# A two-layer model block: a new order of tiles in the last mixers, a merged set-up, weights made ready early, and a swapped product in the forgetting attention

## The chip, the cores and the metric

The kernel runs on one core of a Trainium2 chip. The metric is the device time of one execution in microseconds (us). A profile holds one execution. TensorE is called PE (its weight loads PEld), VectorE DVE, ScalarE ACT, GpSimd POOL, and SyncE, which here issues the DMAs, SP.

## What is computed

Two blocks over one sequence of 2048 tokens, model width 1024, all float32. The first block projects the input to 4652 columns, runs five mixers (spatial gating, forgetting attention, mLSTM, RWKV-7, memory attention) and projects back. The second projects to 3784 columns, runs two mixers and ends with a projection, a residual and a layer norm. What the change touches, from the reference:

```python
# forgetting attention, per block of 128 queries and head
s = einsum("bthd,bshd->bhts", qb, k) * scale + fb[..., :, None] - big_f[..., None, :]
p = softmax(where(k_pos <= q_pos, s, -inf));  out = einsum("bhts,bshd->bthd", p, v)
...
# second block, sparse attention, per block of 128 queries
dots = einsum('bqhd,bsd->bqhs', iqb, ik) * idx_scale               # index scores, 8 heads
score = einsum('bqh,bqhs->bqs', iwb * w_scale, relu(dots))         # -inf where not admissible
_, sel = top_k(score, 256)
logits = einsum('bqhr,bqkr->bqhk', ql, c_sel) * scale + bias;  o = einsum(softmax(logits), c_sel)
# second block, HGRN2, scanned over chunks:  o and state from q, k, v, cumulated log gates
...
y = einsum('bsc,cd->bsd', concatenate([o_a, o_b]), w_o)
x = layer_norm(ALPHA * x + y, ln_g, ln_b)
```

## The kernel before

**Steps.** The program is a row of blocks (`step`), each with a barrier of all engines at its end. Inside a step the work is written as branches, and each branch is a generator per engine that yields places between 0 and 1. `together` merges the branches of one engine by these places into one fixed order. An engine works in that order strictly, so an instruction that waits holds up everything of its engine that stands behind it. SP's order is written in the same way; waits for stores of the step before stand at its head.

**The last mixers** (`second_mixers`, line 3296). The sequence is 16 tiles of 128 queries. Tile t sees the keys of tiles 0 to t, so its cost grows with its width W = 128 (t+1). Four parts follow one another for each tile, each in a later step:

- `index_scores`: per index head and piece of 512 keys a matmul (L2651), a Relu on ACT (L2635) and a multiply-add on DVE (L2614), in two PSUM banks in turn.
- `upper_half`, on DVE alone: sixteen rounds that bisect the upper 16 bits of the 256th largest score, each a counting pass over W (L2714) and two small operations. Tiles 0 and 1 have no more than 256 keys and skip it.
- `lower_half`: sixteen rounds on ACT for the lower 16 bits, each a Sign pass over W with a sum (L2754) and two small ones; then on DVE, from place 0.66 on and behind a wait for ACT's last round (L2773), a chain of passes over W that makes the selection mask (L2774 to L2804).
- `attend`: logits (L2995), masked sum and maximum on DVE (L2933), exponentials on ACT, transposes (L3001), their copies on ACT, and the weighted sum (L3008) for 4 heads; at the end a product with w_uv and a gate.

Beside them `hgrn_chunk` works one chunk of the HGRN in steps 0 to 15, forwards in time, a long chain over all engines (seven levels, POOL, ACT, PE and DVE in turn).

Tiles go from 15 down to 0. Step k has index 15-k, upper half 16-k, lower half 17-k and attention 18-k, so 19 steps work, and a 20th stores the last rows. Buffers for scores rotate by `k % 3`, the others by `k % 2`. Before the loop stand a load step, a step that norms c, forms the table of relative biases and transposes c and the index keys (L3330 to L3369), two steps for the HGRN's lower bound (`hgrn_setup`), one that sets a constant, and one that waits for the first tiles. The bias table is loaded from memory in step 0 and mirrored by four matmuls in step 1.

**The last projection** (`project_out` with a layer norm, line 2323) loads w_o in 8 pieces of 128 rows through three slots and splits each into a high and a low part (L2461 on ACT, L2484 on DVE). Each output tile takes 48 matmuls (L2417 to L2419) of 128x512. The first two tiles are computed piece by piece as the weights come. On SP the columns of the third tile are queued behind all the weights' loads.

**The forgetting attention** (`fox_attend`, line 1199) runs for one tile of queries per step beside the two halves of an RWKV chunk, whose triangular inverse (L2154, blocks of 64x64) is the last thing in most steps. Per head and piece of 512 keys: logits (L1298), maximum on DVE (L1272), Exp on ACT, 128x128 transposes (L1315), copies (L1257), and in `weigh` (L1322) the product of the transposed probabilities (stationary, 128x128) with the values (moving, 128x64), summed in PSUM.

## Time and profile before

| | |
|---|---|
| median of 3 runs | 5283.35 us |
| lowest, highest | 5280.79, 5286.9 us |
| profiled execution | 5289.84 us |
| its span | 5288.2 us |
| busy share PE / DVE / ACT / POOL | 83% / 51% / 36% / 13% |
| granted TensorE clock, mean | 0.827 |

A busy share is a mean over stages. Whether an engine sets the time has to be read stage by stage: from a table of busy times in a stretch, and from what stands idle before an instruction and what released it. The timeline view merges neighbouring instructions of a kind into one row; the time from one row's start to the next one's start is what these instructions cost on their engine. A matmul of float32 has two records, a transpose one.

### The profile page before, as it was taken

Reading aid. Unit: us, or ns where it says so; the run is one execution under the profiler, and the core shown is the slowest. Engines: PE = TensorE matmul, PEld = TensorE weight load, DVE = VectorE, ACT = ScalarE, POOL = GpSimd, SP = SyncE. Lnnn points to the kernel's source line nnn. Section 1 sums busy time; section 2 is a strip of 40 time slices with the busy share of each in tenths; the row PEclk is TensorE's granted clock in tenths of the full one; section 3 lists DMA queues with packets and bytes.
Section 4 is the critical chain, followed back from the end, with each engine's and each line's share of the span. In section 5 each row is a group of like instructions: output and inputs, shape, how many; then the busy total and the mean of one; then the engine's idle time right before and its main releaser. Section 6 shows DMA issues by size and latency. Waiting matters only on the chain. (4 is left out here: it accounts for less than half of the span.)

```text
span 5288.2 us, 65270 instructions
## 1 busy us (share of the span) xinstructions
PE 4384.3 (83%) x23498; PEld 3313.7 (63%) x23498; DVE 2679.4 (51%) x5418; ACT 1921.6 (36%) x3904; POOL 712.9 (13%) x745
## 2 busy tenths in 40 slices
PE   7997899983578888898899999956688887876679
PEld 6876777772466666676787888833344444544567
DVE  3114444454555544544212111138988888887546
ACT  3112232333323323333102010113677767777621
POOL 3111111100000000000000000012223333434400
PEclk9998999985677767767899999976577887878779
DMA  5337666653000000000423212120000001011033
GB/s 181 117 120 240 206 219 216 200 183 129 28 23 24 23 23 23 23 12 5 166 96 115 82 68 76 55 61 23 18 19 19 19 19 37 19 37 37 24 126 116
DMA packets 203971, 426.38 MB, mean 81 GB/s; under 512 B 37544, under 2 KB 67916, under 8 KB 203484
## 3 DMA queue, kind: packets, MB, share of 16 engines
q1 hardware_dynamic: 203648, 422.20, 23.2%
q8 instruction: 187, 3.06, 0.2%
q14 instruction: 136, 1.11, 0.1%
HBM read 300.47 MB, written 121.65 MB: 80 GB/s over the span
## 5 line engine op out<-in xcount | busy, mean ns | idle before, releaser
L3162 POOL TENSOR_TENSOR ds_E<-ds_bT 128x256 f32<-128x256 f32 x112 | 72.9, 651 | 2869.0 <-ACT ds_bT L3131 2683.6
L2651 PE MATMUL ds_big<-ds_ikT,ds_iqT 64*128 64x512 f32 (+3 forms) x640 | 378.0, 740 | 90.2 <-ACT ds_iqT L2628 56.5
L301 PE MATMUL g_acc<-g_ws_hi,g_hT_hi 128*128 128x512 f32 (+1 forms) x1024 | 386.9, 378 | 0.0
L303 PE MATMUL g_acc<-g_ws_hi,g_hT_lo 128*128 128x512 f32 (+1 forms) x1024 | 385.3, 376 | 0.0
L302 PE MATMUL g_acc<-g_ws_lo,g_hT_hi 128*128 128x512 f32 (+1 forms) x1024 | 385.2, 376 | 0.0
L2714 DVE TENSOR_SCALAR_CACHE_REDUCE ds_eq<-ds_hi,ds_num 128x2048 uint16<-128x2048 uint16 (+13 forms) x224 | 331.3, 1479 | 25.7 <-issue 3.5
L529 PE MATMUL mm_big<-mm_gw_hi,mm_ghT_hi 128*128 128x512 f32 (+1 forms) x768 | 318.5, 415 | 30.4 <-PEq L134 30.4
L530 PE MATMUL mm_big<-mm_gw_lo,mm_ghT_hi 128*128 128x512 f32 (+1 forms) x768 | 300.2, 391 | 0.0
L531 PE MATMUL mm_big<-mm_gw_hi,mm_ghT_lo 128*128 128x512 f32 (+1 forms) x768 | 300.2, 391 | 0.0
L2754 ACT ACTIVATE ds_signs<-ds_lo,ds_at 128x2048 bf16<-128x2048 uint16 (+13 forms) x224 | 291.3, 1300 | 1.2
L328 DVE COPY g_stage<-g_acc 128x512 f32<-128x512 f32 (+1 forms) x64 | 41.5, 649 | 459.2 <-PE g_acc L303 459.2
L2651 PEld LDWEIGHTS ds_big<-ds_ikT,ds_iqT 64*128 64x128 f32 x640 | 110.9, 233 | 238.3 <-issue 83.7
L2614 DVE SCALAR_TENSOR_TENSOR ds_score<-ds_rel,ds_iw,ds_score 128x512 f32<-128x512 f32 (+3 forms) x280 | 227.6, 817 | 62.6 <-ACT ds_rel L2635 43.2
L1298 PE MATMUL fox_big<-fox_kT,fox_qT 65*128 65x512 f32 (+3 forms) x320 | 223.0, 791 | 25.5 <-PEq L134 25.5
L2635 ACT ACTIVATE ds_rel<-ds_big 128x512 f32<-128x512 f32 (+3 forms) x320 | 167.6, 528 | 189.7 <-PE ds_big L2651 89.6
L3270 PEld LDWEIGHTS ds_big<-ds_E 128*128 128x128 f32 x896 | 137.4, 234 | 140.0 <-issue 74.8
L1257 ACT ACTIVATE fox_pT<-fox_big 128x512 f32<-128x512 f32 (+3 forms) x160 | 85.2, 533 | 371.5 <-PE fox_big L1315 371.4
L347 ACT ACTIVATE g_stage<-g_acc 128x512 f32<-128x512 f32 (+1 forms) x64 | 36.2, 565 | 502.5 <-PE g_acc L303 502.5
L303 PEld LDWEIGHTS g_acc<-g_ws_hi,g_hT_lo 128*128 128x128 f32 x1024 | 193.8, 189 | 35.5
L302 PEld LDWEIGHTS g_acc<-g_ws_lo,g_hT_hi 128*128 128x128 f32 x1024 | 193.9, 189 | 34.8
L301 PEld LDWEIGHTS g_acc<-g_ws_hi,g_hT_hi 128*128 128x128 f32 x1024 | 194.0, 189 | 34.7
L3270 PE MATMUL ds_big<-ds_E 128*128 128x128 f32 x896 | 158.7, 332 | 67.1 <-POOL ds_E L3169 39.4
(512 smaller groups left out, 10307.8 us busy)
## 6 DMA issues: line engine op xcount, KB each, us to landing
mm_ghT_hi<-turned SPq DMA_DIRECT2D x96, 512.0 KB, 4.1
mm_ghT_lo<-turned SPq DMA_DIRECT2D x96, 512.0 KB, 5.4
proj<-g_stage SPq DMA_DIRECT2D x112, 256.0 KB, 2.0
proj<-mm_gstage SPq DMA_DIRECT2D x80, 256.0 KB, 5.0
mm_x<-proj SPq DMA_DIRECT2D x64, 256.0 KB, 3.9
second_raw<-in_w_in SPq DMA_DIRECT2D x56, 256.0 KB, 4.1
proj<-fp_stage SPq DMA_DIRECT2D x48, 256.0 KB, 2.0
mm_graw<-in_w_in SPq DMA_DIRECT2D x40, 256.0 KB, 6.5
```

Source lines behind the costliest of these rows:

```text
L301: pe.matmul(sums, hT.hi[:, k, tile], wt.hi[:, k, 0:width], start=(k == 0), stop=False)
L302: pe.matmul(sums, hT.hi[:, k, tile], wt.lo[:, k, 0:width], start=False, stop=False)
L303: mm = pe.matmul(sums, hT.lo[:, k, tile], wt.hi[:, k, 0:width], start=False, stop=(k == KD - 1))
L529: pe.matmul(sums, b.hT.hi[:, u % 3, k], wt.hi[:, k, 0:width], start=(k == 0), stop=False)
L530: pe.matmul(sums, b.hT.hi[:, u % 3, k], wt.lo[:, k, 0:width], start=False, stop=False)
L531: m = pe.matmul(sums, b.hT.lo[:, u % 3, k], wt.hi[:, k, 0:width], start=False, stop=(k == KD - 1))
L1298: pe.matmul(big[:, n, 0:wd], b.qT[:, h, k * P:(k + 1) * P], b.kT[:, h, x:x + wd], start=True, stop=True).then_inc(s.logits, 1)
L2614: d = dve.scalar_tensor_tensor(out=score[:, x:x + wd], in0=rel[:, n % 2, 0:wd], scalar=sg, in1=score[:, x:x + wd], op0=ALU.mult, op1=ALU.add)
L2651: pe.matmul(big[:, n % 2, 0:wd], iqT[o, h // 2], b.ikT[o, x:x + wd], start=True, stop=True)\
L2714: dve.tensor_scalar(seen, hi, cand, 0.0, ALU.is_ge, ALU.add, accum_out=count)
L2754: act.activation(signs, lo, ACT.Sign, bias=now, accum_out=sums[:, bit:bit + 1])
L3270: m = pe.matmul(big[:, 6 + l % 2, h * P:(h + 1) * P], E[:, l % 2, h], E[:, l % 2, h], start=True, stop=True)
```

## The change

1. **Order of tiles.** `ATTENDED = [1, 0, 9, 15, 3, 14, 4, 13, 5, 12, 6, 11, 7, 10, 8, 2]`; `SCORED` is the same without tiles 1 and 0, which take all their keys and are no longer scored. Step k has index SCORED[k] (k < 14), upper half SCORED[k-1], lower half ATTENDED[k], attention ATTENDED[k-1]. From the third entry on lower half and attention are those of SCORED[k-2] and SCORED[k-3]. 17 steps work and an 18th stores. Buffers rotate by the place in the order (`PLACE`).
2. **Set-up.** One step (`last_mixers_setup`) does what the load step and the five steps behind it did; the copy of the transposed index keys moves from DVE to ACT, in two halves. The bias table's load and its mirroring are both in step 0.
3. **Weights of the last projection.** In step 16, beside the attention of tile 2, `last_weights` loads and splits w_o into buffers that take the place of the index, threshold and HGRN buffers. `project_out` gets them as `held`, leaves out its own loads and asks for columns and rows at once.
4. **Forgetting attention, k >= 4.** `weigh` has the values as the stationary operand (64 columns) and the probabilities as the moving one (128 columns). Even key tiles sum in partitions 0 to 63, odd ones in 64 to 127 of PSUM bank 7. At the end ACT copies the sums, and four matmuls with a fold matrix (two identities one above the other) add the halves and turn them back.

```diff
+FOLDED = 4
@@ fox_attend
+        if folded:
+            yield 11 / N
+            act.wait_ge(s.f_weighed, HEADS * NP)
+            act.activation(pT[:, 0], sums, ACT.Copy).then_inc(s.f_sums_kept, 1)
...
+        if folded:
+            yield 11 / N
+            take(pe, "o")
+            pe.wait_ge(s.f_sums_kept, 1)
+            for h in range(HEADS):
+                m = pe.matmul(o[:, h], pT[:, 0, h], b.fold[:], start=True, stop=True)
+            m.then_inc(s.f_folded, 1)
...
+            at = x // P + t
+            v, w = b.v[:, at, h * HD:(h + 1) * HD], pT[:, (h * NP + p) % 2, t]
+            if folded:
+                m = pe.matmul(sums[(LOW, HIGH)[at % 2], h], v, w, start=(at < 2), stop=(at + 2 > k))
+            else:
+                m = pe.matmul(o[:, h], w, v, start=(at == 0), stop=(at == k))
@@ the order
+SCORED = [9, 15, 3, 14, 4, 13, 5, 12, 6, 11, 7, 10, 8, 2]
+ATTENDED = list(range(PLAIN - 1, -1, -1)) + SCORED
+PLACE = {t: n for n, t in enumerate(ATTENDED)}
@@ last_mixers_setup, PE
+            pe.wait_ge(s.ik_in, 32)
+            for t in range(8):
+                m = pe.transpose(big[:, 5 + t // 4, (t % 4) * P:(t % 4 + 1) * P],
+                                 ik[:, t].rearrange("p r d -> p (r d)"), c.ident)
+            m.then_inc(s.ik_t, 1)
+            pe.wait_ge(s.oh_in, 32)
+            for k in range(5):
+                m = pe.matmul(big[0:HEADS, k], rb, oh[:, k * 512:(k + 1) * 512], start=True, stop=True)
+            m.then_inc(s.biases, 1)
+            pe.wait_ge(s.bias_kept, 1)
...
@@ last_weights
+        for k in range(D_MODEL // P):
+            yield 0.01 * k
+            if k >= 3:
+                sp.wait_ge(s.pw_lo, k - 2)
+            sp.dma_start(b.x[:, k % 3], w_out[k * P:(k + 1) * P, :]).then_inc((s.pw_in0, s.pw_in1, s.pw_in2)[k % 3], 16)
...
+            yield 0.1 + 0.11 * k
+            act.wait_ge((s.pw_in0, s.pw_in1, s.pw_in2)[k % 3], 16 * (k // 3 + 1))
+            act.activation(b.ws.hi[:, k], b.x[:, k % 3], ACT.Copy).then_inc(s.pw_hi, 1)
...
+            yield 0.15 + 0.11 * k
+            dve.wait_ge(s.pw_hi, k + 1)
+            dve.tensor_tensor(b.ws.lo[:, k], b.x[:, k % 3], b.ws.hi[:, k].bitcast(F32), ALU.subtract)\
+               .then_inc(s.pw_lo, 1)
@@ second_mixers
-        order = list(range(TILES - 1, -1, -1))
-        for k in range(TILES + 4):
+        for k in range(TILES + 2):
+            if k == TILES:
+                early.close()
+                last.x = B.sb("px", [P, 3, D_MODEL])
+                last.ws = Split(B, "pws", [P, D_MODEL // P, D_MODEL])
...
+                if k < N:
+                    branches.append(index_scores(c, ib, s, proj, big, order[k]))
+                if 1 <= k <= N:
+                    branches.append(upper_half(c, tb, s, order[k - 1]))
+                if k < TILES:
+                    branches.append(lower_half(c, tb, s, attended[k]))
+                if 1 <= k <= TILES:
+                    branches.append(attend(c, ab, s, proj, big, attended[k - 1], after))
+                if k == TILES:
+                    branches.append(last_weights(last, s, w['w_o_2']))
```

## Rows read from the trace of the kernel before

**Rows 1.** The page: granted TensorE clock in tenths, 40 slices of the span.

```profile
PEclk9998999985677767767899999976577887878779
```

**Rows 2.** Stages: stretch, length, busy PE, PEld, DVE, ACT, POOL, clock, DMA share, GB/s.

```profile
3464.30:3523.00 58.70, 13.91 (x42) 6.08 (x42) 24.58 (x18) 1.58 (x3) 0.00 (x0) 0.57 0.32 79
3523.00:5060.80 1537.80, 1163.53 (x4712) 707.90 (x4712) 1255.70 (x2468) 1015.58 (x2081) 533.25 (x608) 0.76 0.07 25
5063.40:5288.20 224.80, 197.82 (x896) 163.49 (x896) 125.92 (x168) 35.09 (x73) 0.00 (x0) 0.93 0.37 136
1598.10:2504.00 905.90, 798.91 (x6240) 609.89 (x6240) 443.50 (x1104) 286.11 (x540) 0.00 (x0) 0.72 0.06 19
```

**Rows 3.** Same view: loop steps 0, 1, 3, 3 to 12, 15, 16.

```profile
3523.00:3590.10 67.10, 51.74 (x176) 25.79 (x177) 39.53 (x55) 32.60 (x65) 30.38 (x34) 0.78 0.10 36
3590.10:3695.10 105.00, 70.00 (x184) 34.11 (x184) 91.25 (x134) 32.45 (x64) 29.68 (x34) 0.61 0.05 16
3803.60:3928.90 125.30, 107.66 (x420) 61.62 (x420) 113.11 (x189) 88.57 (x156) 34.69 (x38) 0.76 0.05 18
3803.60:4796.90 993.30, 793.17 (x3356) 481.26 (x3357) 873.27 (x1706) 715.22 (x1408) 339.37 (x380) 0.80 0.07 24
4934.40:4996.50 62.10, 41.79 (x204) 31.83 (x204) 29.53 (x66) 44.23 (x120) 31.58 (x38) 0.75 0.09 30
4996.50:5022.20 25.70, 19.48 (x64) 13.60 (x64) 6.57 (x22) 8.39 (x17) 3.98 (x4) 0.53 0.12 41
```

**Rows 4.** Same view: step 3 split at DVE's start on the lower half.

```profile
3803.60:3896.20 92.60, 80.32 (x256) 42.08 (x257) 82.61 (x144) 74.53 (x123) 27.51 (x33) 0.69 0.07 24
3896.20:3928.90 32.70, 27.33 (x167) 19.54 (x164) 30.50 (x47) 14.04 (x33) 7.18 (x6) 0.96 0.00 1
```

**Rows 5.** Lines 2754, 2774 in step 3: ns min/median/max, first and last start.

```profile
L2754 ACT ACTIVATE ds_signs<-ds_lo,ds_at x16: 1879/1886/1907, 3810.0 to 3882.2; 128x1920 bf16<-128x1920 uint16 x16
...
L2774 DVE CAST ds_num<-ds_kept x1: 142/142/142, 3896.2 to 3896.2; 128x1 uint16<-128x1 f32 x1
```

**Rows 6.** Group by line and shape, loop: busy us, mean ns, idle before.

```profile
L2714 DVE TENSOR_SCALAR_CACHE_REDUCE ds_eq<-ds_hi,ds_num 128x2048 uint16<-128x2048 uint16 x16 | 37.5, 2346 | 1.8 <-issue 0.2
```

**Rows 7.** Line 1322, steps k>=4: PE, PEld, clock; PE's timeline, k=15.

```profile
1598.10:2504.00 905.90, 149.98 (x1008) 148.03 (x1008) 0.72 0.06 19
...
2462.95 1.00 PE L1322 MATMUL fox_big<-fox_v,fox_pT 128*128 128x64 f32 x8
2463.79 0.65 PE L1298 MATMUL fox_big<-fox_kT,fox_qT 65*128 65x512 f32 x1
...
2475.72 0.60 PE L1315 MATMUL fox_big<-consts_sb,fox_L 128*128 128x128 f32 x4
2476.16 1.00 PE L1322 MATMUL fox_big<-fox_v,fox_pT 128*128 128x64 f32 x8
2477.09 0.68 PE L2154 MATMUL fox_big<-fox_X,fox_G 64*64 64x64 f32 x16
2477.70 0.70 PE L1298 MATMUL fox_big<-fox_kT,fox_qT 65*128 65x512 f32 x1
...
2499.26 0.68 PE L2154 MATMUL fox_big<-fox_ex,fox_XT 64*64 64x64 f32 x16
2499.77 0.63 PE L2154 MATMUL fox_big<-fox_XT,fox_ex 64*64 64x64 f32 x16
```

**Rows 8.** Set-up: landing of ct's load; timeline row of the reciprocal.

```profile
DMA to landing us min/median/max: 7.8/7.8/7.8
...
3511.06 3.35 DVE L3058 RECIPROCAL ds_lb<-ds_lb 128x512 f32<-128x512 f32 x1
```

**Rows 9.** Timeline: start us, length, engine, line; first products of last projection.

```profile
5072.98 0.79 PE L2417 MATMUL pf_acc<-pf_ws_hi,pf_mS_hi 128*128 128x512 f32 x1 [0.56 <-DVE pf_mS_lo L2478]
...
5087.84 0.80 SPq L2367 DMA_DIRECT2D pf_x<-x  x2
...
5094.42 1.97 PE L2411 MATMUL pf_tp<-consts_sb,pf_m 128*128 128x128 f32 x8 [8.57 <-DMA pf_m<-mixed]
```

More of the change, by code:

```diff
@@ L1078, in fox_rwkv_and_gating @@
         fb.qT, fb.kT, fb.v, fb.z = qT, kT, v, B.sb("z", [P, 2, GW])
+        fb.fold = B.sb("fold", [P, HD])
         rb = rwkv_early_buffers(B)
@@ L1083, in fox_rwkv_and_gating @@
             ub = sgu_buffers(nc, c, E, w)
-            with step(nc, "sgu_in gains_in ahead_in turned masked scaled cleared") as (block, s):
+            with step(nc, "sgu_in gains_in ahead_in turned masked scaled cleared folds") as (block, s):
                 @block.sync
@@ L1105, in _ @@
                     dve.memset(carry[:], 0.0).then_inc(s.cleared, 1)
+                    dve.tensor_tensor(fb.fold[:], c.ident[:, LOW], c.ident[:, HIGH], ALU.add).then_inc(s.folds, 1)
                     dve.wait_ge(s.gains_in, 48)
@@ L1205, in fox_attend @@
     NP = len(PIECES)
-    o = big[:, 7, 0:GW].rearrange("p (h d) -> p h d", h=HEADS)
+    sums = big[:, 7].rearrange("p (h t) -> p h t", h=HEADS)
+    folded = k >= FOLDED
     N = 12.0
@@ L2458, in _ @@
                 keep(0)
-                for k in range(K):
+                if held:
+                    keep(1)
+                for k in range(0 if held else K):
                     act.wait_ge(w_in[k % 3], 16 * (k // 3 + 1))
@@ L2481, in _ @@
                 rest(0)
-                for k in range(K):
+                if held:
+                    rest(1)
+                for k in range(0 if held else K):
                     dve.wait_ge(s.w_hi, k + 1)
@@ L2526, with bias_flip @@
 BIAS_SIGNALS = "bias_in flipped flip_kept "
-def bias_load(bias, s, table):
+def bias_flip(c, bias, s, big, table):
     def sync(sp):
@@ L2670, in threshold_buffers @@
     return b
-def threshold_setup(nc, b):
-    with step(nc, "start_set") as (block, s):
-        @block.vector
-        def _(dve):
-            dve.memset(b.at[:, 2:3], -32767.5).then_inc(s.start_set, 1)
 SELECT_SIGNALS = "low_found "
@@ L2695, in upper_half @@
     cand, hit, n_hi = (cell(n) for n in range(3))
-    top, need, level = (b.kept[:, k % 2, n:n + 1] for n in range(3))
+    top, need, level = (b.kept[:, PLACE[k] % 2, n:n + 1] for n in range(3))
     KEEP = float(TOPK)
@@ L2871, in sync @@
         sp.dma_start(gate[:].rearrange("p h d -> p (h d)"), proj[tok, E_G:E_G + H * P]).then_inc(s.g_in, 16)
-        if k:
-            n = attend_loads(b, sp, s.q_ahead, proj, k - 1)
+        if after is not None:
+            n = attend_loads(b, sp, s.q_ahead, proj, after)
             yield 1.0
@@ L3301, in second_mixers @@
+LAST_SIGNALS = "pw_in0 pw_in1 pw_in2 pw_hi pw_lo "
+def second_mixers(nc, c, w, proj, mix, table, onehot, x_old, out):
     H, R, KEEP = 4, 128, float(TOPK)
+    order, attended, N = SCORED, ATTENDED, len(SCORED)
     with ExitStack() as ctx:
@@ L3450, in _ @@
                     together(pe, "tensor", branches)
+        banks.close()
+        project_out(nc, c, mix, w['w_o_2'], x_old, out, "pf", ln=(w['ln_g_2'], w['ln_b_2']), held=last)
 def program(nc, t, consts, onehot, out):
```

324 lines of the change are left out of this document (165 added, 159 removed).

## Prediction

> **What bounds the kernel now.** I read the page's clock line first: the granted TensorE clock changes from stage to stage, so this is a chain of stages with limits of their own [rows 1]. Then the table by stage [rows 2]: the set-up of the final mixers takes 58.7 us, their loop 1537.8 with DVE busier than PE (1255.7 against 1163.5), the last projection 224.8, and the forgetting-attention steps that the change touches 905.9, of which PE is busy 798.9. Then the loop by its steps [rows 3], which I number 0 to 18 (a store step of 2.6 us follows). In steps 1 to 12 DVE is busy all but some 10 to 14 us, as 113.1 of 125.3 in step 3, or 873.3 of 993.3 in steps 3 to 12 together. Steps 0 and 15 have little for DVE (39.5 and 29.5) and still take 67.1 and 62.1: a floor which the chain of one HGRN chunk sets. Steps 16 to 18 do nothing but the attention of tiles 2, 1, 0; the last two end the loop and take 38.6 us together [rows 2, 3]. Last, step 3 split at the instruction with which DVE takes up the lower half [rows 4, 5]: before it DVE is busy 82.6 of 92.6 us, behind it 30.5 of 32.7. ACT had ended its 16 passes at 3884 (the last starts at 3882.2), 12 us before DVE came to them at 3896.2. ACT's chain is covered by DVE's own work, by 12 us, and the new order spends that margin.
>
> **A model of one step, tried on the old ones.** DVE takes a step's work in a written order: the whole upper half, two thirds of the rest, then the lower half's tail among the last third. So a step is the later of two prefixes plus a suffix. I added the durations of each branch's instructions in every step; they are nearly linear in the tile number t. DVE: upper half 21 (t=2) to 53 us (15), lower half 7 to 15, index 8 (t=0) to 31, attention 5 to 16, HGRN 10.3. ACT: lower half 22 (t=2) to 44, index 3 to 20, attention 6 to 21, HGRN 16.3. The counting passes carry most of the slopes: 16 of 2.35 us on DVE for tile 15 [rows 6], 16 of 1.89 on ACT for tile 14 [rows 5]. With R the sum of index, attention and HGRN on an engine: DVE prefix = upper + 0.66 R + 5; ACT prefix = lower + 0.60 R + 3; suffix = DVE's lower + 0.34 R + 1.5. The constants are read off the splits of the old steps. For old step 3 that is 88.2 + 34.4 = 122.6 against 125.3, for steps 3 to 12 together 992 against 993.3 [rows 3].
>
> **The loop in its new order.** Step k has index SCORED[k], upper half SCORED[k-1], lower half SCORED[k-2], attention SCORED[k-3]. So wide upper half and wide attention meet in even steps, wide index and wide lower half in odd ones. Even, step 4 (index 4, upper 14, lower 3, attention 15): DVE prefix 51.7 + 27 + 5 = 83.7, ACT prefix 53.6, suffix 22.5: 106.2. Odd, step 5 (index 13, upper 4, lower 14, attention 3): DVE prefix 25.6 + 28.5 + 5 = 59.1, but ACT prefix 42.6 + 25.6 + 3 = 71.2. So DVE stands 12 us at the lower half, with index sums, HGRN picks and attention queued behind it; suffix 31.6: 102.8. Steps 2, 3 and 6 to 14 give by the same sum 96.8, 111.4, 104.7, 102.0, 104.4, 97.7, 102.2, 97.5, 102.9, 85.9, 75.5. Step 1 is DVE's sum of 87 us and the 10 by which old step 1 is over its own: 97. Steps 0 and 15 are at the floor, 64 and 66 [rows 3]. Steps 0 to 15 make 1517. The attention of tiles 1 and 0 lies in steps 1 and 2 at no cost of its own, and the index of tiles 0 and 1 is gone; the price is that DVE waits for ACT in odd steps and that both ends are thinly filled. Step 16 has the attention of tile 2 (25.7 [rows 3]) beside the last weights. In the last projection these were done 24 us after its start (5063.4 to 5087.84, where SP's wait for them ends [rows 2, 9]). Here they start some 4 us late, behind the store wait at the head of SP's queue, and share ACT and DVE: I take 34.5, between 28 and 42. Loop: 1551.5 against 1537.8, **+14 us**. Bounds: -19 if ACT's prefix never binds (every step its DVE sum plus 6.5 us, the mean excess of old steps 3 to 12), +35 if the even steps also run out of PE in their short suffix: PE is busy 27.3 of 32.7 us behind the split of step 3 [rows 4], and a suffix of 22.5 us must hold nearly the same attention.
>
> **The set-up** becomes one step; before it was two rounds of loads, three short steps and a round of arrivals. ct lands at about 11.6 us (issued third, 7.8 us to land as before [rows 8]). PE forms the bias table from 16 to 24.6, DVE copies it by 27.4, the transposes of ct end at 33, their copy at 35.6, and the lower bound's chain behind it (a reciprocal of 3.35 [rows 8] and five short ones) near 42. With the block's edges 43: **-16 us**, between -22 and -10. The flips of the bias table move from step 1 into step 0, whose 64 has them.
>
> **The last projection** starts with its weights ready. PE's first product came at 5072.98, 9.6 us into the step, and later PE stood 8.57 us until 5094.42, since the third tile's columns were queued on SP behind all weight loads [rows 9]. The second stall goes whole, of the first 2.5 us, and less idle time means fewer products at the low clock. **-12 us**, between -15 and -8. What is late next is PE itself, 197.8 us [rows 2].
>
> **The forgetting attention** changes for k of 4 and more: 12 steps, 504 products of probabilities and values, 1008 PE records, PE busy 150.0 us with them [rows 7]. Each now loads 64 columns of weights and streams 128, and neighbours write to different halves of the partitions. At the full clock 8 records of the old form take 0.84 us and 4 transposes, which stream 128 columns, 0.44 [rows 7]: 105 to 110 ns a record either way. So if nothing runs side by side there is no gain, and if pairs do, half. No row shows two column halves over all 128 rows. The nearest is L2154, 64 x 64 blocks on the diagonal: 16 records in 0.51 us [rows 7], 32 ns each, where half of 110 is needed to stream 64 columns alone. I take full overlap: -75. Against it: the last matmul of an odd count runs alone (+4). Each of 144 groups changes the array's shape twice: entering costs 0.09 us (8 records 0.93 ahead of L2154, 0.84 ahead of L1298), leaving 0.10 (L2154 0.61 instead of 0.51) [rows 7]: +29. The closing fold has 8 more records a step (+14), and its wait for ACT's 0.6 us copy stands ahead of the last inverse levels, which end the step (+6). Net -22 on PE, which is busy 88% of the stage: **-19 us**, between -55 (switches hidden) and +46.
>
> The Trainium skill speaks on both sides here. Its page TensorEngine Tiling (Array Packing), section Performance Considerations, advises this very exchange of stationary and streaming operand with two column tiles where the streamed dimension is 64 or less; by it the term would stay as above. Its page TensorE: Matmul & The Clock Gate, section The mechanism, says that a weight load overlaps running matmuls only where the row group differs; by it the term would be that of the first rival. No row here shows this shape.
>
> **Sum.** -16 + 14 - 12 - 19 = -33. The profiled execution took 5289.84 us, its span is 5288.2; less 33 that is 5257. The median of the three runs is 5283.35, so the forecast is **5250 us**, 0.6% faster.
>
> **Rivals.**
> First, the column halves do not run side by side, because both load and stream over the same 128 rows. For: the only concurrent rows differ in row half too. Against: L2154's blocks also write to different column halves and lose nothing by it. Price: the gain of 75 goes, the switches, folds and waits remain, +46 instead of -19, total 5315, slower. It decides from a pitch of about 96 ns a record in the mean of both clocks (today 149): above that the edit loses. Chance 0.15.
> Second, ACT's prefix stays hidden and each step is DVE's sum plus 6.5: loop -19, total 5217. For: ACT's work in step 5 (85 us) fits into 91. Against: DVE waits at one fixed place of its order. Chance 0.18.
> Third, the alternation costs more: in even steps PE ends the suffix, in odd ones both engines lose: loop +35, total 5271. For: PE at 27.3 of 32.7 [rows 4]. Chance 0.17.
> Fourth, the change doesn't do what it says: the small tiles lengthen steps 1 and 2 by what they took alone, 5283. Against: DVE needs 5 us for each, beside 80 of other work. Chance 0.04.
> The forecast: 0.46.
>
> **Range and chances.** The forecast's own range is 5222 to 5276. With the second and third rival and a part of the first, 8 in 10 is 5200 to 5305. A measurement of this kernel can tell about 0.2% from no change: faster means under 5272.8, slower over 5293.9. Faster 0.74 (forecast 0.44, second 0.18, third 0.10, the rest 0.02), same 0.12, slower 0.14.
>
> **What would show it.** In the loop, DVE idle some 12 us ahead of the lower half in step 5, released by ACT, and even steps near 104. The set-up one step of about 43. In the last projection the first product within 7.5 us and no stall at the third tile. In the forgetting attention, records of the weighted sum in pairs, their PE time near 75, the stage near 887. I am wrong if that time stays near 150, if DVE is busy throughout odd steps, or if step 16 is over 42.

## The result, and the profile after

The changed kernel takes 5312.78 us (median of 5 runs, 5307.27 to 5314.62) against 5283.35 us (5 runs, 5280.16 to 5290.55): a ratio of 1.0052, with a 95% interval of 1.0038 to 1.0067. It is slower by half a per cent. I had forecast 5250 us, with a range of 5200 to 5305. The result is outside that range and on its other side.

The stages, as in [rows 2] (columns: stretch, length, busy PE, PEld, DVE, ACT, POOL, clock, DMA share, GB/s): set-up, loop, last projection, and the twelve forgetting-attention steps with k of 4 and more.

```profile
3460.30:3501.90 41.60, 16.31 (x42) 7.51 (x42) 22.39 (x17) 3.43 (x6) 0.00 (x0) 0.51 0.45 112
3501.90:5096.50 1594.60, 1189.81 (x4672) 721.99 (x4672) 1237.42 (x2448) 1019.13 (x2071) 532.60 (x608) 0.73 0.08 27
5099.10:5311.20 212.10, 193.77 (x896) 160.44 (x896) 116.23 (x160) 26.85 (x65) 0.00 (x0) 0.95 0.33 124
1604.10:2501.00 896.90, 766.87 (x6336) 536.17 (x6336) 442.52 (x1104) 291.91 (x552) 0.00 (x0) 0.73 0.06 19
```

| stage | before | after | difference | forecast |
|---|---|---|---|---|
| set-up | 58.7 | 41.6 | -17.1 | -16 |
| loop | 1537.8 | 1594.6 | +56.8 | +14 |
| last projection | 224.8 | 212.1 | -12.7 | -12 |
| forgetting attention, k >= 4 | 905.9 | 896.9 | -9.0 | -19 |
| all else | | | +5.0 | 0 |
| span | 5288.2 | 5311.2 | +23.0 | -33 |

Two stages came out as worked out, one gave half of its gain, and the loop alone turned the sign. What is under "all else" is in stages that the change does not touch: step k = 4 of the forgetting attention began at 1598.1 us before and at 1604.1 after, and between 1594 and 1613 us over the profiles of this study.

In the loop DVE has 18 us less to do than before (1237.4 against 1255.7) and the loop is 57 us longer. So it is waiting that grew: DVE is idle for 357.2 us of the loop, where it was idle for 282.1. The same view by steps, against [rows 3]: steps 0, 4, 5 and 16, and step 5 split at the instruction with which DVE takes up the lower half.

```profile
3501.90:3572.60 70.70, 57.77 (x168) 29.31 (x168) 32.16 (x53) 26.69 (x56) 26.71 (x34) 0.64 0.10 34
3883.70:3993.80 110.10, 79.80 (x388) 53.01 (x388) 93.58 (x173) 61.49 (x140) 33.58 (x38) 0.81 0.06 22
3993.80:4108.90 115.10, 91.59 (x252) 48.54 (x252) 82.20 (x165) 77.90 (x144) 33.40 (x38) 0.60 0.06 21
5064.10:5096.50 32.40, 17.42 (x64) 11.73 (x64) 14.92 (x28) 15.94 (x25) 5.96 (x4) 0.63 0.46 154
3993.80:4074.90 81.10, 67.84 (x154) 33.27 (x154) 52.73 (x124) 67.27 (x116) 25.55 (x32) 0.52 0.09 30
4074.90:4108.90 34.00, 23.75 (x99) 15.28 (x98) 29.47 (x43) 10.63 (x28) 7.84 (x7) 0.80 0.00 0
```

The even step 4 is a step as DVE had them before: busy 93.6 of 110.1. The odd step 5 is not: DVE is busy 82.2 of 115.1, and 28 us of its idle time lie before the lower half. There I had expected one wait of 12 us, right at the lower half. The two instructions in question, in step 5 (durations in ns min/median/max, first and last start), as in [rows 5]:

```profile
L2783 ACT ACTIVATE ds_signs<-ds_lo,ds_at x16: 1879/1886/1897, 4000.2 to 4063.3; 128x1920 bf16<-128x1920 uint16 x16
...
L2803 DVE CAST ds_num<-ds_kept x1: 150/150/150, 4074.8 to 4074.8; 128x1 uint16<-128x1 f32 x1
```

ACT's last pass starts at 4063.3 and its chain is over at 4065.9, 72.1 us into the step; I had worked out 71.2. DVE comes to the lower half only at 4074.8, 9 us later, and nothing holds it there. It is late because it had been held earlier. The waits of step 5 (engine, line waited for, us in total, times, longest), first DVE's, then ACT's:

```profile
DVE ds_score L2652 <- ACT ds_rel L2673: 13.5, 9, 3.2
DVE ds_score L2656 <- ACT ds_rel L2673: 5.2, 2, 3.9
```

```profile
ACT ds_rel L2673 <- PE ds_big L2689: 14.2, 7, 3.4
ACT ds_rel L2673 <- DVE ds_score L2652: 7.0, 5, 3.7
```

The index branch is a chain over three engines: PE forms a product (L2689), ACT takes its Relu (L2673), DVE adds it to the scores (L2652, L2656), through two PSUM banks and two SBUF places. In odd steps the index is wide (tiles 14, 13, ...) and so is the lower half, whose Sign passes stand on ACT between the Relus. A few microseconds of step 5, in order of time (start, length, engine, line; in brackets the idle time before it and who ended it):

```profile
4010.30 2.07 PE L2689 MATMUL ds_big<-ds_ikT,ds_iqT 64*128 64x512 f32 x2
...
4013.99 0.59 ACT L3122 ACTIVATE ds_kT<-ds_big 128x512 f32<-128x512 f32 x1
...
4014.47 1.89 ACT L2783 ACTIVATE ds_signs<-ds_lo,ds_at 128x1920 bf16<-128x1920 uint16 x1
...
4017.31 0.60 ACT L2673 ACTIVATE ds_rel<-ds_big 128x512 f32<-128x512 f32 x1
...
4017.94 0.49 DVE L2656 TENSOR_SCALAR ds_score<-ds_rel,ds_iw 128x512 f32<-128x512 f32 x1 [3.95 <-ACT ds_rel L2673]
```

The product is there at 4012.4 (one product is two records). ACT takes its Relu at 4017.3. Ahead of it in ACT's order stand work of the HGRN chunk (a table load of 1.28 us and three short instructions, of which the last is shown) and a Sign pass of 1.89 us with its short followers. DVE stands 3.95 us for it. Over the whole loop the waits of the index sums for a Relu more than doubled. First before, then after:

```profile
DVE ds_score L2614 <- ACT ds_rel L2635: 43.2, 28, 3.8
...
DVE ds_score L2618 <- ACT ds_rel L2635: 7.7, 6, 3.8
```

```profile
DVE ds_score L2652 <- ACT ds_rel L2673: 90.3, 60, 4.0
...
DVE ds_score L2656 <- ACT ds_rel L2673: 19.5, 8, 4.2
```

That is 50.9 us before and 109.8 after: 59 of the 75 us by which DVE's idle time grew. In steps 3, 5, 7, 9 and 11 together DVE waits 62.2 us for Relus, in steps 4, 6, 8, 10 and 12 10.0 us; in the loop before, the same steps had 8.6 and 3.6.

### The profile page after: what moved, and what is told of

The parts are those of the page before. It is cut to its first block and busy times, and to the rows that moved or that the text cites. A ratio compares the mean times of both kernels' runs of the same rounds, so it can differ in the third digit from the quotient of the medians.

```text
span 5311.2 us, 65208 instructions
## 1 busy us (share of the span) xinstructions
PE 4382.9 (83%) x23554; PEld 3258.4 (61%) x23554; DVE 2646.5 (50%) x5390; ACT 1924.2 (36%) x3900; POOL 714.0 (13%) x745
## 5 line engine op out<-in xcount | busy, mean ns | idle before, releaser
L2689 PE MATMUL ds_big<-ds_ikT,ds_iqT 64*128 64x512 f32 (+3 forms) x608 | 393.8, 793 | 75.2 <-ACT ds_iqT L2666 55.6
L2743 DVE TENSOR_SCALAR_CACHE_REDUCE ds_eq<-ds_hi,ds_num 128x1280 uint16<-128x1280 uint16 (+13 forms) x224 | 331.3, 1479 | 25.0 <-issue 2.6
L2783 ACT ACTIVATE ds_signs<-ds_lo,ds_at 128x1280 bf16<-128x1280 uint16 (+13 forms) x224 | 291.3, 1300 | 1.4
L2652 DVE SCALAR_TENSOR_TENSOR ds_score<-ds_rel,ds_iw,ds_score 128x512 f32<-128x512 f32 (+3 forms) x266 | 210.0, 791 | 106.2 <-ACT ds_rel L2673 90.3
L3264 PEld LDWEIGHTS ds_big<-ds_E 128*128 128x128 f32 x896 | 149.6, 251 | 159.0 <-POOL ds_E L3163 81.7
L3264 PE MATMUL ds_big<-ds_E 128*128 128x128 f32 x896 | 170.1, 349 | 72.5 <-POOL ds_E L3163 44.5
L2689 PEld LDWEIGHTS ds_big<-ds_ikT,ds_iqT 64*128 64x128 f32 x608 | 108.3, 241 | 196.5 <-issue 73.6
L2673 ACT ACTIVATE ds_rel<-ds_big 128x512 f32<-128x512 f32 (+3 forms) x304 | 162.9, 538 | 174.3 <-PE ds_big L2689 123.8
L301 PEld LDWEIGHTS g_acc<-g_ws_hi,g_hT_hi 128*128 128x128 f32 x1024 | 193.8, 189 | 34.8
```

Of the source, the lines that this page charges most:

```text
L301: pe.matmul(sums, hT.hi[:, k, tile], wt.hi[:, k, 0:width], start=(k == 0), stop=False)
L2652: d = dve.scalar_tensor_tensor(out=score[:, x:x + wd], in0=rel[:, n % 2, 0:wd], scalar=sg, in1=score[:, x:x + wd], op0=ALU.mult, op1=ALU.add)
L2689: pe.matmul(big[:, n % 2, 0:wd], iqT[o, h // 2], b.ikT[o, x:x + wd], start=True, stop=True)\
L2743: dve.tensor_scalar(seen, hi, cand, 0.0, ALU.is_ge, ALU.add, accum_out=count)
L2783: act.activation(signs, lo, ACT.Sign, bias=now, accum_out=sums[:, bit:bit + 1])
L3264: m = pe.matmul(big[:, 6 + l % 2, h * P:(h + 1) * P], E[:, l % 2, h], E[:, l % 2, h], start=True, stop=True)
```

## The experiments

All kernels below are the changed kernel with one edit or two. The kernel before was run on the same chip beside each group; its medians there were 5291.6 (first four), 5292.4 (next four) and 5287.6 us (last four), and a ratio is against those. Where no interval or range is given (experiments 2, 3, 5 and 6, and the first run of 7), the time is that of one execution, and every figure of a stage or step is that of one profile.

**1. The change taken apart: order and fold.** The first run leaves the forgetting attention in its old form, the second gives the fourteen scored tiles in falling order as before the change (tiles 1 and 0 still ahead of them), the third does both.

```diff
-FOLDED = 4
+FOLDED = 16
```

> The changed kernel with the forgetting attention as before (FOLDED = 16, nothing else). Theory A (the loop alone makes the kernel slower, the fold still earns a little): the 12 attention steps go from 896.9 back to some 906, the total rises by 5 to 20 us over the changed kernel, to 5318 to 5333. Rival B (the fold costs what it saves on PE, since the inverse's chain and the fold's own wait end the step, and the clock falls): the total moves by less than 8 us either way. Rival C (the fold is the loss): the total falls by 10 to 30 us and the changed kernel without it is as fast as before.

```diff
-SCORED = [9, 15, 3, 14, 4, 13, 5, 12, 6, 11, 7, 10, 8, 2]
+SCORED = list(range(TILES - 1, PLAIN - 1, -1))
```

> The changed kernel with the tiles scored from wide to narrow, 15 down to 2, behind tiles 1 and 0 (SCORED descending, nothing else), so that the small tiles still fill the early steps but no wide index meets a narrow upper half. Theory A (the alternation is the loss: in odd steps DVE waits for Relus in the index ring): steps 3 to 13 return to the lengths of before (1066 us together), the loop with its step 16 is 1510 to 1525 us instead of 1595, the total 5225 to 5245, ratio to before 0.989 to 0.993. Rival B (the filled early steps and the merged buffers are the loss, not the alternation): the loop stays above 1570 and the total within 20 us of the changed kernel.

> Both edits: descending order and no fold. If the two parts add up, the total is that of the descending order plus what the run without the fold shows against the changed kernel. Theory A: 5235 to 5260. Rival B (the fold costs what it saves): within 8 us of the descending order alone. Rival C (the fold is a loss): 10 to 30 us below it.

("fox" is the forgetting attention with k of 4 and more.)

| | new fold | old form |
|---|---|---|
| alternating order | 5312.8 (loop 1594.6, fox 896.9) | 5327.5 (1594.4, 910.0) |
| falling order | 5239.0 (1526.6, 896.9) | 5246.6 (1526.6, 910.0) |

Ratios: no fold 1.0079 (1.0058 to 1.0101), falling order 0.9899 (0.9881 to 0.9918), both 0.9930 (0.9906 to 0.9953). The alternation costs 68 us of loop, and the rest of the change (small tiles in the early steps, short set-up, weights loaded early, fold) is worth 1% with the old order. Over all profiles of this study the alternating loop took 1594.4 to 1598.6 us (three) and the falling one 1512.3 to 1526.6 (four), so that 68 is at the low end. By the medians the fold earns 8 us in the falling order and 15 in the alternating one, where the two kernels were run in different groups (against their own medians of the kernel before it is 6.5). The intervals with and without it overlap in both orders, and its stage, 13 us shorter here, was not always so (experiment 7). The loop in falling order:

```profile
3498.20:5024.80 1526.60, 1181.38 (x4672) 712.68 (x4672) 1242.22 (x2448) 1017.43 (x2071) 534.23 (x608) 0.75 0.08 28
```

DVE's sum for the loop is the same within 5 us in both orders (1237.4 and 1242.2), ACT's within 2. The order moves no work, it only moves waiting: at L2652 DVE waits 52.4 us for Relus in the falling order (41.0 in a second profile), 90.3 in the alternating one. Waits for Relus are not all of it. DVE also waits longer for the attention's logits, first in falling, then in alternating order:

```profile
DVE ds_L L2962 <- PE ds_big L3024: 28.2, 24, 3.2
```

```profile
DVE ds_L L2962 <- PE ds_big L3024: 53.0, 32, 5.8
```

That is in steps 14 and 15, where the alternating order has the attention of tiles 10 and 8 and the falling one that of 4 and 3: DVE waits 39 us for logits there against 7, and the two steps take 145.2 us against 123.0. This part of the price stood in the forecast (75.5 and 66 us).

**2. How the loss grows with the contrast.** An order that steps down in mild turns.

```diff
-SCORED = [9, 15, 3, 14, 4, 13, 5, 12, 6, 11, 7, 10, 8, 2]
+SCORED = [15, 9, 14, 8, 13, 7, 12, 6, 11, 5, 10, 4, 3, 2]
```

> The changed kernel with the order 15, 9, 14, 8, 13, 7, 12, 6, 11, 5, 10, 4, 3, 2 after tiles 1 and 0: alternation with a width difference of six tiles instead of up to twelve. Theory A (the loss grows with the mismatch of wide index and lower half against the narrow upper half): the loop is between the descending order's 1526.6 us and the alternation's 1594.6, near 1560. Rival B (a constant cost of alternating, or of the first steps): 1590 or more. Rival C: as the descending order, 1535 or less.

Measured 5284.41 us, loop 1562.1: about halfway between 1526.6 and 1594.6. So a milder contrast between neighbours costs less. DVE's waits for Relus moved with the wide index, which now stands in even steps: 39.7 us in steps 4 to 12, 3.0 in steps 3 to 11.

**3. Is it ACT's Sign passes?** They read 128 keys instead of up to 2048; their number and order stay. This kernel leaves most keys out of the search for the lower 16 bits, so its selection is another.

```diff
-            act.activation(signs, lo, ACT.Sign, bias=now, accum_out=sums[:, bit:bit + 1])
+            act.activation(signs[:, 0:P], lo[:, 0:P], ACT.Sign, bias=now, accum_out=sums[:, bit:bit + 1])
```

> A timing probe on the changed kernel: ACT's sixteen Sign passes of the lower half read only the first 128 keys of a tile instead of all, so the selection is not that of the reference. It takes 12 to 28 us of ACT work out of every step with a wide lower half. Theory A (in odd steps DVE waits for Relus that stand behind the Sign passes in ACT's order): odd steps 3 to 9 fall from 104 to 118 us to their DVE sum plus 5 to 9, that is to 90 to 98, and even steps move by less than 4. Rival B (the Relus are late because PE runs at the low clock and its index products are late): odd steps fall by less than 5 us and DVE still waits 10 us or more for Relus in step 5.

Measured 5257.91 us; the loop falls from 1594.6 to 1538.7. The odd steps 3 to 11 fall from 547.0 together to 503.4, the even steps 4 to 12 stay at 520.3. DVE's waits for Relus in these odd steps fall from 62.2 us to 20.1, which is 42 of the 44 us. So it is the passes that hold up the Relus. By itself the total could not tell this from ACT's own sum, which my formula had and which short passes take away too; that ACT's sum was not the later one is seen in step 5 of the changed kernel, where DVE came 9 us behind its end. But step 5 came to 105.1, not to the 90 to 98 that I expected: only half of the way. Its rows (whole, then up to DVE's start on the lower half), and the waits of DVE and of ACT in it:

```profile
3986.40:4091.50 105.10, 84.78 (x252) 44.81 (x252) 82.81 (x165) 54.46 (x144) 33.09 (x38) 0.66 0.07 23
3986.40:4057.40 71.00, 61.08 (x154) 29.59 (x154) 53.32 (x125) 43.82 (x116) 25.28 (x32) 0.60 0.10 34
```

```profile
DVE ds_score L2652 <- ACT ds_rel L2673: 6.8, 4, 2.5
...
DVE ds_score L2656 <- ACT ds_rel L2673: 1.6, 1, 1.6
```

```profile
ACT ds_rel L2673 <- PE ds_big L2689: 24.1, 13, 3.4
ACT ds_rel L2673 <- DVE ds_score L2652: 7.6, 6, 3.7
```

DVE's waits for Relus fell from 18.7 to 8.4 us, and ACT now waits 24.1 us for products: behind ACT the next link of the chain is PE.

**4. Is it the depth of the ring?** Three banks and three places in steps 3, 5, 7, 9 and 11, with the products issued a turn earlier.

```diff
-    b.rel = B.sb("rel", [P, 2, 512])
+    b.rel = B.sb("rel", [P, 3, 512])
...
-            if n >= 2:
-                act.wait_ge(s.summed, n - 1)
-            act.activation(rel[:, n % 2, 0:wd], big[:, n % 2, 0:wd], ACT.Relu).then_inc(s.relus, 1)
+            if n >= deep:
+                act.wait_ge(s.summed, n - deep + 1)
+            act.activation(rel[:, n % deep, 0:wd], big[:, n % deep, 0:wd], ACT.Relu).then_inc(s.relus, 1)
...
-            yield place(n - 0.4 * (n % 2))
+            yield place(max(0, n - 0.4 * (n % 2) - (deep - 2)))
...
+            deep = 3 if k in (3, 5, 7, 9, 11) else 2
```

> The changed kernel, but in steps 3, 5, 7, 9 and 11 the index products rotate through three PSUM banks and three Relu buffers instead of two (the narrow attention of those steps gets two banks instead of three), and PE issues each product a turn earlier. Theory A (in odd steps PE, ACT and DVE hold one another up because the ring of index products has two places): odd steps 3 to 11 fall from 547 us together by 20 to 40, the total to 5275 to 5295. Rival B (ACT's own sum, with the wide lower half, sets the pace, whatever the ring): odd steps fall by less than 8 us together.

The attention of these steps has two banks instead of three for it. Measured 5306.73 us, ratio 1.0034 (1.0016 to 1.0051); odd steps 540.4, loop 1590.0. A third place gives 6.6 us of the 36 that the odd steps are over the forecast, and DVE's waits for Relus in them stay, 62.5 us against 62.2. Nor is 6.6 us clear of chance: the three kernels that share the alternating loop word for word (the changed one, the one without the fold and the first of experiment 7) had 547.0, 550.5 and 554.1 us in the odd steps, and 519.0 to 520.3 in the even ones.

**5. Is it the length of the products?** The index matmuls in fp32r.

```diff
-    b.iqT = B.sb("iqT", [P, IDX_HEADS // 2, P])
+    b.iqT = B.sb("iqT", [P, IDX_HEADS // 2, P], F32R)
...
-        ikT, score = E.sb("ikT", [P, SEQ]), E.sb("score", [P, 3, SEQ])
+        ikT, score = E.sb("ikT", [P, SEQ], F32R), E.sb("score", [P, 3, SEQ])
```

> A timing probe on the changed kernel: the index products' operands are kept as fp32r, so a product is one pass instead of two; the scores lose precision and the selection can differ from the reference's. Theory A (PE's late products are a part of the ring's time in odd steps, by its low clock): odd steps 3 to 11 fall by 20 us or more together and ACT's wait for products in step 5 falls from 14.2 us below 7. Rival B (only ACT's Sign passes matter, of which the short-Sign probe already took 44 us of 547): less than 8 us together.

Measured 5297.09 us; odd steps 531.5, even 513.3, loop 1566.1. In step 5 PE sheds 27 us and the step 6.4:

```profile
3990.80:4099.50 108.70, 64.34 (x220) 42.20 (x220) 82.16 (x165) 77.98 (x144) 33.05 (x38) 0.62 0.07 22
```

```profile
DVE ds_score L2652 <- ACT ds_rel L2673: 8.9, 7, 3.2
DVE ds_score L2656 <- ACT ds_rel L2673: 5.2, 2, 3.9
```

```profile
ACT ds_rel L2673 <- DVE ds_score L2652: 8.9, 6, 3.7
ACT ds_rel L2673 <- PE ds_big L2689: 3.5, 4, 1.3
```

ACT's waits for products fell from 14.2 to 3.5 us, and DVE still waits 14.1 for Relus: with long Sign passes the products are not what sets the pace. Over the five odd steps DVE's waits for Relus stay, 61.4 us against 62.2; the steps gain 12 of their 15.5 us from other waits, those for logits among them (5.2 to 0). Neither theory was right here, it is in between. Of the 28 us of loop the odd steps gave 15.5, the even ones 7.0 and step 0, where ACT has few passes to make, 5.3 (70.7 to 65.4).

**6. Two links at once.** Short passes with fp32r products, and short passes with the three-place ring.

> The changed kernel in its alternating order, with ACT's Sign passes reading only the first 128 keys (which leaves most keys out of the lower half's search) and the index products in fp32r (which rounds their operands). Odd steps 3 to 11 together took 547.0 us, 503.4 with short Sign passes alone, 531.5 with fp32r alone. Theory A (the chain product, Relu, sum runs at the pace of its slowest link: ACT while its Sign passes are long, PE behind it): the two together do more than their sum of -59, near 480 us, and in step 5 ACT's waits for products, 24 us with short passes, fall under 8. Theory B (with ACT freed, DVE's written order is what is left): 495 to 503 us, and the sum of the two single effects, 488, is not reached.

> As the run with short Sign passes (which leave most keys out of the lower half's search), and in steps 3, 5, 7, 9 and 11 a ring of three places for index products and Relu outputs with the products one turn earlier. Theory A (the depth of the ring matters once ACT is no longer the slowest link, since it takes the latency of the product out): odd steps 3 to 11 fall from 503.4 to 485 us or less. Theory B (a third place gives what it gave with long passes): 495 to 500 us.

The first took 5225.26 us: odd steps 478.6, loop 1500.2. That is -68 for both edits where they gave -44 and -16 one by one. The second took 5243.91: odd steps 489.0, so that the ring now gives 14.4 us where it gave 6.6 with long passes; my expectation of 485 or less was missed by 4 us. The surplus, 9 us in the first and 8 in the second, is hardly more than the 7 us by which the odd steps of one loop differ between profiles; clearer are DVE's waits for Relus in them, 20.1 us with short passes alone, 7.2 and 13.0 here. Step 5 of the first, whole and up to DVE's start on the lower half, then DVE's waits for Relus and ACT's for sums and products in it:

```profile
3972.00:4067.70 95.70, 65.19 (x220) 43.19 (x220) 84.86 (x165) 54.31 (x144) 34.13 (x38) 0.62 0.07 25
3972.00:4035.30 63.30, 46.79 (x144) 29.48 (x144) 55.10 (x126) 44.17 (x117) 27.75 (x34) 0.60 0.11 38
```

```profile
DVE ds_score L2656 <- ACT ds_rel L2673: 0.8, 1, 0.8
...
DVE ds_score L2652 <- ACT ds_rel L2673: 0.3, 1, 0.3
```

```profile
ACT ds_rel L2673 <- DVE ds_score L2652: 15.9, 9, 4.2
...
ACT ds_rel L2673 <- PE ds_big L2689: 4.1, 4, 1.4
```

DVE waits 1.1 us for Relus instead of 18.7, and ACT waits for DVE: the chain has turned round. DVE is at the lower half after 63.3 us (my forecast of its prefix was 59.1) and the step takes 95.7. This is how an odd step looks in which DVE sets the pace. The excess of the odd steps is thus for the most part DVE's wait for Relus that stand behind ACT's passes. The products and the two places shorten that wait only once the passes are short; what fp32r gave beside long passes came from elsewhere, and whether the ring gave anything there is not shown.

**7. What the column halves side by side are worth.** The operands stay exchanged as in the change, but every key tile sums in the lower partitions, so that no pair in different halves is left. First in the alternating order:

```diff
-                m = pe.matmul(sums[(LOW, HIGH)[at % 2], h], v, w, start=(at < 2), stop=(at + 2 > k))
+                m = pe.matmul(sums[LOW, h], v, w, start=(at == 0), stop=(at == k))
...
-            act.activation(pT[:, 0], sums, ACT.Copy).then_inc(s.f_sums_kept, 1)
+            act.activation(pT[LOW, 0], sums[LOW], ACT.Copy).then_inc(s.f_sums_kept, 1)
...
-                m = pe.matmul(o[:, h], pT[:, 0, h], b.fold[:], start=True, stop=True)
+                m = pe.matmul(o[:, h], pT[LOW, 0, h], c.ident[LOW, LOW], start=True, stop=True)
```

> The changed kernel with the swapped product kept, but all key tiles sum in the lower half of the partitions, so no two neighbours can run side by side; the fold is then a plain turn by four matmuls over 64 rows. Theory A (the swap earns only because two column halves run together): 8 records take 0.86 to 0.92 us at the full clock instead of 0.59, PE time of the line rises from 99.4 to 145 or more, and the 12 attention steps from 896.9 us to 930 to 950, longer than the 909.9 of the kernel without the swap. Rival B (it earns because half as many weight columns are loaded): the steps stay within 8 us of 896.9.

Measured 5301.84 us. The records behave as expected and the stage does not. PE's timeline in step k = 15 at the full clock, the changed kernel first, then this one: eight records of the weighted sum, and the start of what follows them.

```profile
2460.57 0.66 PE L1349 MATMUL fox_big<-fox_pT,fox_v 128*64 128x128 f32 x8
2461.16 0.68 PE L2182 MATMUL fox_big<-fox_X,fox_G 64*64 64x64 f32 x16
```

```profile
2458.30 1.09 PE L1349 MATMUL fox_big<-fox_pT,fox_v 128*64 128x128 f32 x8
2459.31 0.68 PE L2182 MATMUL fox_big<-fox_ex,fox_XT 64*64 64x64 f32 x16
```

Eight records take 0.59 us with the halves in turn and 1.01 in one half. From start to start single records follow at 109 ns in one half; with the halves in turn two records start 7 ns apart, and the pairs follow at 109 ns. So in the change pairs do run side by side. Yet the stage is shorter without them. L1349 alone, then the whole stage of this kernel; the whole stage of the changed kernel stands above.

```profile
1604.10:2501.00 896.90, 99.40 (x1008) 64.65 (x1008) 0.73 0.06 19
```

```profile
1600.50:2486.00 885.50, 140.66 (x1008) 114.76 (x1008) 0.79 0.06 20
...
1600.50:2486.00 885.50, 767.86 (x6336) 559.10 (x6336) 442.52 (x1104) 291.59 (x552) 0.00 (x0) 0.79 0.06 20
```

L1349 costs PE 41.3 us more, and all of PE 767.9 instead of 766.9: the other groups of the stage together took 40 us less, and the granted clock was 0.79 instead of 0.73. Not every step gained: k = 14 and 15 took 86.7 and 86.5 us, where they had taken 82.7 and 85.0. The expectation of a longer stage fell. Since one profile could be chance, the falling order was run again and beside it with the sums in one half:

> The kernel with the whole change and the fourteen scored tiles in falling order, measured a second time, as the partner of the run beside it. Both theories expect 5233 to 5245 us, the loop near 1526 us and the forgetting attention of k >= 4 at 897 us with a granted clock near 0.73.

> Falling order, and in the forgetting attention operands exchanged as in the change, but all sums in the lower partitions, so that no two records run side by side. Theory A (the pairs side by side save PE time, but the stage is granted a lower clock with them, so that the two nearly cancel or more): records again near 1.01 us for eight, stage near 886 us with the clock near 0.79 against 897 and 0.73, and the kernel 8 to 12 us faster than the falling order alone, near 5228 us. Theory B (the 11 us were chance between two executions): stage 897 to 905 us, and the kernel 5239 us or some microseconds more, since the records take 41 us more of PE.

| | us, median | ratio to before | stage | its clock | loop |
|---|---|---|---|---|---|
| falling order, halves in turn | 5242.12 (5231 to 5257) | 0.9907 (0.9882 to 0.9932) | 896.9 | 0.73 | 1512.3 |
| falling order, one half | 5227.87 (5214 to 5234) | 0.9877 (0.9851 to 0.9903) | 885.5 | 0.79 | 1515.3 |

```profile
1603.10:2488.60 885.50, 767.81 (x6336) 559.07 (x6336) 442.68 (x1104) 291.55 (x552) 0.00 (x0) 0.79 0.06 20
```

The stage came out the same to the tenth in both profiles with one half, with the same clock. With halves in turn it took 896.9 us in five profiles, 899.8 in one and 907.0 in three, with a clock of 0.72 to 0.73; in the old form 905.9 to 910.0 in three, with 0.71 to 0.72. So against the old form the pairs gain between nothing and 13 us of stage, and the one half some 20 to 25. The medians of the last two kernels differ by 14 us, though the two intervals overlap. The last kernel is the fastest that computes the whole selection in float32, 1.2% under the kernel before.

## Why the prediction was wrong, step by step

- **Set-up, right.** One step of 41.6 us, forecast 43.
- **Last projection, right in its sum and half right in its reason.** 212.1 us, -12.7 against -12. PE's start of the transposes of the first tile, the first product, and the transposes of the third tile, as in [rows 9]:

```profile
5102.90 1.97 PE L2442 MATMUL pf_tp<-consts_sb,pf_m 128*128 128x128 f32 x8 [7.47 <-DMA pf_m<-mixed]
...
5108.02 0.79 PE L2448 MATMUL pf_acc<-ds_pws_hi,pf_mS_hi 128*128 128x512 f32 x1 [0.56 <-DVE pf_mS_lo L2512]
```

```profile
5121.51 1.03 PE L2442 MATMUL pf_tp<-consts_sb,pf_m 128*128 128x128 f32 x8
```

The third tile (5121.51) has no stall left, as said. The first product comes 8.9 us into the step, where I had said within 7.5: that part gave 0.7 us, since PE still waits 7.5 us for the first columns. PE's own time in the stage fell by 4.1 us (197.8 to 193.8), at a clock of 0.95 instead of 0.93. The weights were loaded early, but the columns are asked for only when the stage starts. Those of the first tile are stored from step 3 on, so the data would allow an earlier load; no run tries it.

- **Step 16, right**: 32.4, forecast 34.5.
- **Even steps, right in the sum, with luck**: steps 4 to 12 took 520.3 together, forecast 520.4. One by one they missed by +3.9, +1.7, -1.2, -2.0 and -2.5 us, which cancels. The rival in which PE ends their short suffix fell.
- **Odd steps, the term that failed.** Steps 3 to 11 took 547.0, forecast 511.4, and step 0 took 70.7, forecast 64. These two are 42 of the 43 us by which the loop missed. The step of my working was "DVE prefix 59.1, but ACT prefix 71.2", a maximum of two sums. ACT's sum was right (72.1). DVE's was not: 81.1 us. I had made it from DVE's instructions and a constant of 5 us for all its waits, read off the old steps, in which a wide index met a lower half about as wide and DVE had 83 us of its own work in 93. In the new odd steps DVE has 53 us of work there and ACT 67. The index sums, which are DVE's own instructions, are paced by the Relus between ACT's passes, and a constant cannot follow that. A maximum at one meeting point is right only if the two engines do not meet before it, and here they meet at each of the index sums. Of my three signs of being wrong (L1349 near 150, DVE busy throughout odd steps, step 16 over 42) none came; I had named none for a DVE that waits longer than 12 us.
- **What the rule would have said of the other order.** With the same formula the falling order comes to 1508 us and the mild turns to 1524, by an estimate made after the result from the durations of the kernel before; measured were 1512 to 1527 in four executions, and 1562. So the formula itself, wrong by 43 us for the alternation, already held that alternating costs some 43 us against the falling order. I applied it only to the change as a whole, against the old loop, and so never saw that one part of the change was a loss. The gain of the other part, placing tiles 1 and 0 in the early steps, hid it: the loop in falling order is 11 to 26 us shorter than before.
- **Forgetting attention: the records as said, the stage wrong.** At the full clock, in step k = 15, a record follows the last one after 112 ns in the old form and 109 in one half, and a pair follows a pair after 109: 105 to 110 and half of it, as I had taken. What was dearer is the start of a group. Its second record comes 160 ns after the first in one half and the second pair 153 ns after the first, where in the old form the second record came after 58. So L1349 fell by 50.6 us (150.0 to 99.4), where my 75, less 4 for odd counts and 13 for entering (144 times 0.09), is 58. All of PE fell by 32.0 (798.9 to 766.9). I had 28, for the 6 us of the copy's wait in my net of 22 are no work of PE: two errors, in the start of a group and in the rest of switches and folds, nearly cancelled. (The switches were also added up as 29 where 144 times 0.19 us is 27.) But the stage shrank by 9.0 only, since PE's idle time rose from 107.0 to 130.0. The waits for ACT's copy ahead of the inverse levels went from 58.9 to 65.5 us and those of the first logits of a step from 14.8 to 24.8:

```profile
PE fox_big L2182 <- ACT fox_ex L2087: 65.5, 42, 3.8
PE fox_big L1315 <- PEq L134: 24.8, 12, 2.1
```

The first, +6.6, is about the 6 us that I had for the copy. The second, +10.0, I had put at nothing: it is PE's wait from its last work to the start of the next step. PE's last record of a step is now the fold (L1332). Behind it DVE has two multiplications and the last merge of the inverse, and the next step starts 2.1 us after PE's end instead of 1.2, in each of the twelve steps. DVE's wait for the fold:

```profile
DVE fox_y L1303 <- PE fox_big L1332: 27.0, 12, 3.4
```

In the old form DVE did not wait ahead of this instruction (L1286) in any of the twelve steps. "PE is busy 88% of the stage, so 22 us of PE are 19 of the stage" was the failing step, with the fold at the step's end priced as PE's work and one copy alone. No run moved the fold to an earlier place. What PE does in a window that ends in a wait for another engine is not worth its share.

- **The first rival, that column halves do not run side by side, fell**: 0.59 against 1.01 us for eight records. By the Trainium skill's page TensorEngine Tiling (Array Packing), section Performance Considerations, this exchange of operands with two column tiles is the thing to do; the trace agrees on the records (0.59 against 1.01 us), while the stage was 11 us shorter with one column tile. The Trainium skill's page TensorE: Matmul & The Clock Gate, section The mechanism, has a weight load overlap running matmuls only where the row group differs. I had derived the first rival's loss from that, and it is the derivation that failed, not the rule. In the trace the loads of the two halves start together, as the matmuls do, and a pair takes the 109 ns of a single record; whether a load overlaps a matmul is shown by no run here.
- **The rival that came nearest in the loop** was my third, "the alternation costs more", whose +35 us had its reason in the even steps and was 22 too small; its total of 5271 us was still faster than before. Its remark that in odd steps "both engines lose" was the true part, and I gave it no price. My 0.14 for "slower" rested mostly on the first rival, which fell.

**What stays open.** The excess of step 0 (70.7 against 64) was not split further than by fp32r products (65.4). Its trace names two parts: DVE waits 6.3 us for the products that mirror the bias table, which I had put into this step at no cost, and 28.8 for Relus, where step 0 before had 21.2 with a much wider index. With both links short the odd steps are still some 11 us over DVE's sum each, where I had called 6.5 the mean; which of it is the ring's was not taken apart. Why the clock is granted higher with one column half is not known, only that it was so in two profiles of two, against nine with halves in turn and three of the old form.

## What to carry to other kernels

When an engine takes instructions of a chain that another engine paces, add up the pacing engine's work between its links. A sum of the waiting engine's own work plus a constant holds only for the mix of work from which the constant was read. Pairing a wide piece of one branch with a narrow piece of another evens out sums, but it can put the wide ends of two branches that share an engine into the same step; look at which engine they share before changing the order. What is put at the end of a step holds up everything that other engines still have to do behind it, so price it there and not as a share of busy time. And price each part of a change against leaving that part out, not only the whole against before: here one line of the change cost 68 us or more, and the rest of it earned 1%.

## What the chip showed that I had not expected

The form of one matmul went with another clock for the whole stage. With its 1008 records in alternating column halves the stage was granted 0.73 of the full clock and PE was busy 766.9 us; with the same records in one half 0.79 and 767.9, though the records themselves took 99.4 and 140.7 us. In this kernel PE's time in a stage was therefore not the sum of its groups at fixed prices: one group became 41 us dearer and the others together 40 us cheaper, and the stage was 11 us shorter.

It would be wrong to read this as a price of pairs. The old form, without pairs, was granted 0.71 to 0.72, no more than the form with them. It is the exchanged form in one half that stands out, with a stage 20 to 25 us shorter than the old form's, of which its own records (140.7 us against 150.0) explain only 9.
